# Norms in half-row pieces, second-block constants computed in the last FFN, conditioning rows turned by TensorE, and first projections that start bank by bank

## The reference

```python
def rms_norm(x, g):
    y = x * rsqrt(mean(x * x, -1) + 1e-6)
    return y * g

for l in range(2):                                   # first block
    proj = rms_norm(x, norm_mix_pre[l]) @ w_in[l]    # 1024 -> 3072, four mixers on its slices
    mix = concat([conf, stick_breaking, retention, short_conv]) @ w_out[l]
    x = x + rms_norm(mix, norm_mix_post[l])
    f = conv_ffn(rms_norm(x, norm_ffn_pre[l]), ffn_up[l], ffn_conv_w[l], ffn_down[l])
    x = x + rms_norm(f, norm_ffn_post[l])

mod  = silu(c) @ ada_w + ada_b                       # second block: 6 x 1024 values
modc = silu(c_ctx) @ ada_w + ada_b
u  = rmsnorm(x, norm1_g) * (1 + sc1) + sh1
uc = rmsnorm(ctx, norm1_g) * (1 + sc1c) + sh1c
y  = token_mixer(u, uc, ...)                         # mLSTM and differential attention
x  = x + g1 * y
x  = x + g2 * moe(modulate(rmsnorm(x, norm2_g), sh2, sc2))   # 32 experts, top 4
return rmsnorm(x, final_norm_g)
```

## Time and profile before

| what | value |
|---|---|
| median of 3 runs | 2182.85 us (2179.92 to 2186.36) |
| the profiled execution | 2183.95 us |
| its span | 2182.2 us |
| PE busy | 2061.6 us, 94% of the span |
| DVE, ACT busy | 867.3 us (40%), 595.2 us (27%) |
| mean granted clock of TensorE | 0.981 |
| chain that ended last | PE 78%, DMA 13%, DVE 4%, issue 2%, ACT 2% |
| loads of expert weights | 95 of 4096 KB, 19.0 us each to landing |

### The profile page before, as it was taken

One profiled execution on the slowest core, in us unless ns is written; L12 is line 12 of the kernel. 1 busy time (PEld: TensorE's weight loads), 2 busy tenths in 40 slices (PEclk: granted clock), 3 DMA queues, 4 the chain that ended last, 5 costly groups with the idle time before them and its releaser, 6 DMA issues.

```text
span 2182.2 us, 27676 instructions
## 1 busy us (share of the span) xinstructions
PE 2061.6 (94%) x11094; PEld 1323.7 (61%) x11094; DVE 867.3 (40%) x1510; ACT 595.2 (27%) x962; POOL 11.6 (1%) x23
## 2 busy tenths in 40 slices
PE   8999999999998998899989999999999999999998
PEld 7869998959995776677789533333333333333332
DVE  6847676947675226553622311111111111111111
ACT  4545555445555323342431100000000000000001
POOL 0000000010000000000000000000000000000000
PEclk9999999999998999999999999999999999999999
DMA  7335553355546534021234699999999999999996
GB/s 293 114 135 200 182 174 141 140 171 192 185 163 231 240 148 162 30 78 52 84 116 154 261 413 413 432 432 432 432 431 431 429 431 432 432 432 432 432 432 291
DMA packets 43237, 589.71 MB, mean 270 GB/s; under 512 B 5185, under 2 KB 5873, under 8 KB 9825
## 3 DMA queue, kind: packets, MB, share of 16 engines
q1 hardware_dynamic: 41392, 583.09, 65.5%
q0 software_dynamic: 1456, 5.01, 0.8%
q10 hardware_dynamic: 288, 0.24, 0.0%
HBM read 587.27 MB, written 1.05 MB: 270 GB/s over the span
## 4 chain that ended last, share of the span: by engine, by line
PE 78%; DMA 13%; DVE 4%; issue 2%; ACT 2%; DVEq 0%; SPq 0%; ACTq 0%
PE psum L1869 46%; PE psum L2299 22%; DMA slots<-exp_w_dram 12%; PE psum L2244 3%; PE psum L2336 3%; PE psum L2411 3%; DVE split_weights L1443 1%; DMA slots<-w_in_dram 0%; DMA slots<-ffn_up_dram 0%; DVE work L1569 0%; PE psum L1889 0%; PE psum L2177 0%; DVE work L1586 0%; DVE split_rows L1246 0%; ACT work L1079 0%
## 5 line engine op out<-in xcount | busy, mean ns | idle before, releaser
L2299 PE MATMUL psum<-slots,work 128*64 128x512 f32 x3072 | 687.2, 601 | 47.8 <-DMA slots<-exp_w_dram 46.3
L2299 PEld LDWEIGHTS psum<-slots,work 128*64 128x64 f32 x3072 | 219.9, 138 | 479.8 <-issue 467.1
L1869 PE MATMUL psum<-split_rows,split_weights 128*128 128x256 f32 (+1 forms) x3744 | 489.8, 293 | 13.0 <-DVE split_rows L1495 4.1
L1869 PEld LDWEIGHTS psum<-split_rows,split_weights 128*128 128x128 f32 x3744 | 473.0, 193 | 33.3 <-issue 12.3
L1268 DVE TENSOR_TENSOR split_weights<-slots,split_weights 128x1024 fp32r<-128x1024 f32 x180 | 219.6, 1224 | 161.3 <-ACT split_weights L923 160.6
L923 ACT ACTIVATE split_weights<-slots 128x1024 fp32r<-128x1024 f32 x180 | 189.9, 1058 | 216.7 <-PE psum L1869 179.1
L1869 PE MATMUL psum<-split_weights,split_rows 128*128 128x512 f32 x1008 | 232.3, 390 | 1.0 <-DVE split_weights L1443 1.0
L1869 PEld LDWEIGHTS psum<-split_weights,split_rows 128*128 128x128 f32 x1008 | 188.3, 188 | 42.5 <-issue 2.5
L1831 DVE TENSOR_SCALAR work<-psum 128x512 f32<-128x512 f32 x32 | 22.0, 689 | 401.4 <-PE psum L2299 401.4
L1869 PE MATMUL psum<-work 128*128 128x128 f32 (+9 forms) x964 | 152.7, 335 | 19.9 <-DVE work L1605 7.1
L1869 PEld LDWEIGHTS psum<-work 128*128 128x128 f32 (+2 forms) x964 | 124.3, 196 | 50.4 <-issue 36.9
(11 more groups left out here) (249 smaller groups left out, 1333.3 us busy)
## 6 DMA issues: line engine op xcount, KB each, us to landing
slots<-exp_w_dram SPq DMA_DIRECT2D x95, 4096.0 KB, 19.0
slots<-w_in_dram SPq DMA_DIRECT2D x56, 1024.0 KB, 6.1
slots<-ffn_up_dram SPq DMA_DIRECT2D x44, 1024.0 KB, 4.8
slots<-ada_w_dram SPq DMA_DIRECT2D x24, 1024.0 KB, 7.0
slots<-ffn_down_dram SPq DMA_DIRECT2D x20, 1024.0 KB, 4.9
slots<-w_out_dram SPq DMA_DIRECT2D x12, 1024.0 KB, 5.0
slots<-w_branch_a_dram SPq DMA_DIRECT2D x4, 1024.0 KB, 8.1
slots<-w_branch_b_dram SPq DMA_DIRECT2D x4, 1024.0 KB, 5.0
```

Of the source, the lines that this page charges most:

```text
L1869: return nc.tensor.matmul(out_, lhsT, rhs, start=first, stop=last)
L2299: return nc.tensor.matmul(b[rows, :], lhs[:, rows], rhs, start=first, stop=last, skip_group_check=True)
```

## The change

It has these parts:

1. **No hardware loop.** The two layers are written out (`each_layer`), waits go by constants.
2. **Norms by halves.** The last two `w_out` slots are multiplied for tile 0 first and then tile 1, and the last two units of `ffn_down` bank by bank, so the banks are completed one after another. Squares are taken on 512 columns (`square_of_bank`, `square_of_sum`); the gain is multiplied before the root is known (`times_gain`), and the inverse root, scaling and addition to `x` are one operation (`add_to_x`).
3. **Turned rows by tile, projection by bank.** `turn` writes each tile to its own four banks, `high_rows` and `low_rows` work on 128x128 pieces in `TILE_ORDER`, and the first unit of a projection waits only for the two chunks that it multiplies next.
4. **Work moved into the last FFN.** The silu of the conditioning vectors, the context norm and the products `ada(0)` and `ada(1)` come ahead of the last two units of layer 1's FFN.
5. **Conditioning rows turned.** Rows 0 to 3 and 6 to 9 go through four 128x128 transposes each, and DVE sums the four partial rows (`mod_columns(n)`). `mq` starts at the first of the eight pieces (`u_ready`), with unit splits 1 and 2 placed between the pieces.
6. **Fewer units ahead.** Before a norm only two units of the next stage are split (`MIX_UNITS + 1`), or one (`splits[l + 1](0)`), instead of three.

The diff, cut to its core:

```diff
@@ constants
-LAYER_BANKS = [("T", i, i) for i in range(4)]
+LAYER_BANKS = [("T", i, i) for i in range(8)]
-LAYER_BANKS += [("F", i, i) for i in range(4)]
+LAYER_BANKS += [("F", i, i) for i in range(8)]
+TILE_ORDER = ((0, 0), (1, 0), (0, 1), (1, 1), (2, 0), (2, 1), (3, 0), (3, 1))
@@ every engine
-        def loop_layers(eng, layer):
-            with eng.Fori(0, DEPTH) as l:
+        def each_layer(layer):
+            for l in range(DEPTH):
                 layer(l)
@@ ScalarE
+            def half_square(rows, t, half, l):
+                i = 2 * t + half
+                n_squared[0] += 1
+                nc.scalar.activation(flat(soft)[:, 0:512], rows, ACT.Square, accum_out=half_sumsq[:, i:i + 1]
+                                     ).then_inc(half_squared, 1)
+                act.wait_ge(half_squared, n_squared[0])
+                if half == 0:
+                    nc.scalar.activation(half_mean[:, t:t + 1], half_sumsq[:, i:i + 1], ACT.Identity, bias=EPS, scale=1.0 / D)
...
-                split_until(MIX_UNITS + UNIT_BUFFERS - 1)
-                rms_of_banks(l, "M")
-                rms_of_x(l, 2 * l + 2)
+                split_until(MIX_UNITS + 1)
+                load_root_table()
+                for t in range(TT):
+                    for square in (square_of_bank, square_of_sum):
+                        square("M", l, t, 0)
+                        square("M", l, t, 1)
+                        root(t)
@@ VectorE
+            def times_gain(key, gain, t, squared):
+                for half in (0, 1):
+                    cut = slice(512 * half, 512 * half + 512)
+                    dve.wait_ge(half_squared, squared[half])
+                    step(nc.vector.tensor_tensor(xhat[:, t, cut], psum[:, bank_of((key, 2 * t + half)), :], gain[:, cut], ALU.mult),
+                         0, wait=False)
+            def add_to_x(l, n, key, t):
+                inverse_rms(n, t)
+                for half in (0, 1):
+                    cut = slice(512 * half, 512 * half + 512)
+                    nc.vector.scalar_tensor_tensor(out=x[:, t, cut], in0=xhat[:, t, cut], scalar=rinv[:, t:t + 1],
+                                                   in1=x[:, t, cut], op0=ALU.mult, op1=ALU.add
+                                                   ).then_inc(evacuated[bank_of((key, 2 * t + half))], 1)
...
-                add_normed(l, 1, [("M", i) for i in range(4)], mix_row)
-                normalise(l, 2, 2 * l + 2)
+                for t in range(TT):
+                    times_gain("M", mix_row, t, (16 * l + 4 * t + 1, 16 * l + 4 * t + 2))
+                    add_to_x(l, 8 * l + 2 * t + 3, "M", t)
+                    normalise_tile(8 * l + 2 * t + 4, t)
...
+                for t in range(TT):
+                    times_gain("D", ffn_row, t, (16 * l + 2 * t + 9, 16 * l + 3 * t + 10))
+                    add_to_x(l, 8 * l + t + 7, "D", t)
+                for t in range(TT):
+                    normalise_tile(8 * l + t + 9, t)
@@ TensorE, layer
                     for k in range(KC):
+                        if rows_of and k % 2 == 0:
+                            after_evacuation(pe, (rows_of, k // 2), l)
+                            after_evacuation(pe, (rows_of, 4 + k // 2), l)
...
+                if l == DEPTH - 1:
+                    pe.wait_ge(siluc_ready, 1)
+                    ada_product(0)
+                    ada_product(1)
+                pe.wait_ge(ff_ready, l * 11 + 11)
+                for i in range(4):
+                    t, half = divmod(i, 2)
+                    for n in (len(UNITS) - 2, len(UNITS) - 1):
+                        pe.wait_ge(w_split, l * len(UNITS) + (n + 1))
...
@@ TensorE, block 2
-                            ins = mm(b[:, at_:at_ + 2], rows[:, c * P:(c + 1) * P], cst2("pick")[:, 0:2])
+                            ins = nc.tensor.transpose(b[:, c * P:(c + 1) * P], rows[:, c * P:(c + 1) * P], ident)
...
+                        if first and k % 2 == 0:
+                            pe.wait_ge(u_ready, k // 2 + 1)
@@ VectorE, block 2
+                def mod_columns(n):
+                    k0 = 4 * (n if n < 4 else n - 2)
+                    b = take(dve, ("mT", n), l).rearrange("p (c q r) -> p c r q", c=4, q=4)[:, :, 0:2, :]
+                    m = modT[:, k0:k0 + 4, :]
+                    nc.vector.tensor_reduce(m, b, AX, ALU.add).then_inc(evacuated[bank_of(("mT", n))], 1)
+                    after_evacuation(dve, ("mT", n), l)
+                    step(nc.vector.tensor_tensor(m, m, ada_b[:, k0:k0 + 4, :], ALU.add), l, wait=n in (3, 9))
```

359 lines of the change are left out of this document (193 added, 166 removed).

## The result

The changed kernel takes 2146.07 us (median of 4 runs, 2144.13 to 2146.78); the kernel before took 2183.07 us beside it (4 runs, 2179.92 to 2186.36). The ratio is 0.9829, 95% interval 0.9812 to 0.9846: 1.7% faster, clear of the noise, and within the forecast's range of 2138 to 2151. The profiled executions have spans of 2145.0 and 2182.2 us, 37.2 us apart.

What follows compares the result with a forecast made beforehand. PE's progress ahead of a fixed-length expert-weight stream was taken as the bound, with the seams left to gain. Gains of 16.0 + 7.6 + 12.5 + 2.2 + 1.0 = 39.3 us gave a median of 2144 us, range 2138 to 2151.

Steps and rivals of the forecast that it cites:

- Mixers' ends: At both mixers' ends, tile 0's norm hides under tile 1's products and the projection starts earlier: 8.0 us each, 16.0 together.
- (a): At all four seams, first units run at half clock, costing 7 to 14 us together: 2152 us, chance 0.13.
- Layer 0's end: Behind layer 0's feed-forward, loop wait and table load vanish and the first unit ends at E + 11.5: gain 7.6 us.
- Into block 2: From layer 1's feed-forward to `mk`, bound by the fourth unit's split and the next load: gain 12.5 us.
- (b): At the seams, the norm chain is longer through slower pieces, or `ada(1)`'s load is late: 2155 us, chance 0.12.
- Rows 6 to 9: In block 2's conditioning, transposes replace small `pick` products of 3.41 and 1.84 us: gain 2.2 us.
- 1.5 + 0.7: Split of the 2.2 us gain from turning conditioning rows, with transposes partly at the slow spot.
- Start of layer 0: At layer 0's first projection, only the pieces change and the first unit ends about 20.3 instead of 21.3: gain 1.0 us.
- Expert stage: The stream of expert weights stays as long, about 980 us from first load to end, and only starts earlier: 0 us.
- (c): In seams and layers, pieces take 0.20 us and waits need no computed register, so the chain is shorter: 2134 us, chance 0.09.
- (d): The expert stage waits for something other than PE's progress and takes the gain back: 2183 us, chance 0.03.
- (e): In both written-out layers, engines wait for instructions because code doubles, so the kernel is slower: 2190 us, chance 0.03.

Runs made afterwards that it cites:

- experiment 6: Changed kernel, but block 2's first query product waits for all four pieces of turned rows instead of following piece by piece: 2142.98 us.
- 3: Changed kernel, but the mixer's last eight output products go over both tiles together, as in the kernel before: 2149.63 us.
- experiment 4: Changed kernel, but at the two mixers' ends ScalarE squares each whole tile, not halves: 2148.08 us.
- experiment 2: Changed kernel, but the first unit after each of four norms waits for all eight banks of turned rows to be split: 2156.80 us.
- 1: Kernel before with only the loop removed, both layers written out: 2179.17 us, ratio 0.9978.
- 7: Changed kernel, but the split of `mq`'s fourth unit stands behind the sixth of eight pieces of rows, not the eighth: 2142.94 us.
- experiment 12: Changed kernel, but conditioning rows 6 to 9 are brought to columns by small picking products again, not transposes and a sum: 2155.80 us.
- 5: Changed kernel, but block 2's first two conditioning products and their rows' evacuation stand behind the last feed-forward product again: 2149.62 us.
- 8: Changed kernel with seven instead of five fillers between tile turns at mixers' ends and layer 0's end, plus five short ones in `mq`: 2146.47 us.
- experiment 9: Changed kernel, but at layer 0's start one unit's weights, not three, are split ahead of the turned rows: 2142.93 us.
- 10: Changed kernel with `mq`'s fourth split behind the sixth piece and one unit's weights split ahead of layer 0's first rows: 2139.41 us.
- experiment 11: Changed kernel with the earlier `mq` split, one unit split ahead at layer 0's start, and the extra fillers: 2139.35 us, ratio 0.9805 without one outlier.

## Why the prediction was right

Its total, 2144 against 2146.07 us, is right and so are most of its terms, by their own marks. In part that is luck: the start of layer 0 came out 1.8 us short of its term, and the expert stage gave 1.8 us that were no effect of the change.

- **Mixers' ends** (16.0 forecast, 13.6 measured). The mechanism holds to the mark: turn at E + 5.3, first unit from E + 7.2. The twelve pieces behind the turn came 0.27 us apart, as taken (3.20 us on VectorE). The first unit ended at E + 11.8 where the prediction has 10.5, and before at E + 19.0 where it has 18.5. The loss is the clock: rival (a) came true at these two places. In the profiles where it stayed at 1.00 the first unit ended 1.0 us earlier behind the turn (5.47 against 6.47 us, experiment 6), which gives 8.2 for layer 0. Of each end, the tiles' order is 1.5 us (3), the halves 1.35 (4), the following 2.4 to 3.9 with what the clock did there (2).
- **Layer 0's end** (7.6, measured 7.8). The sum was right, my reading of its parts was not: the loop's issue and table loads, which looked like the largest part, give 2.0 us of start and 0.55 net by themselves (1). The following gives 2.9 (2). The rest, some 3 to 4 us, would be the norm by halves, the products bank by bank and the fewer units split ahead; these were not tried apart.
- **Into block 2** (12.5, measured 11.6). `mk` hung on the fourth split and its load, as said (6, 7): from the last feed-forward product to `mk` it took 36.2 us (685.69 less 649.45), where the prediction has 36.9. What the term left out is the wait of 1.09 us for the second conditioning product's load (part of rival (b)): the two products took 4.86 us (643.85 less 638.99) and not 3.64.
- **Rows 6 to 9** (2.2, measured 3.3, 4.9 by experiment 12). The step "1.5 + 0.7" is right for the products themselves; it left out the conditioning products behind the first of them, which before ran in the stretch at the lower clock: 5.33 us for 32 products at 782.68 us, 3.66 in the kernel after.
- **Start of layer 0** (+1.0, measured -0.8). This step failed. It has the first unit's end at 20.3 us in place of 21.3; it was 22.08 in place of 21.60. The prediction left the clock out here. In the kernel before, six fillers stood behind the turns and TensorE then waited 1.61 us; after the change they are gone and it waits 3.16 us:

```profile
12.78 4.04 PE L1869 MATMUL psum<-const 128*128 128x384 f32 x12
```

  The clock was at its lower level from about 16 to 23 us, and before not at all. The profile of experiment 4, with the same start code, shows the term without that fall: the first unit ends at 20.27 us, as forecast, and the 192 products at 40.4, which would be +1.3.

```profile
16.69 23.70 PE L1940 MATMUL psum<-split_rows,split_weights 128*128 128x256 f32 x192 [3.61 <-DVE split_rows L1300]
20.27 1.06 ACT L957 ACTIVATE split_weights<-slots 128x1024 fp32r<-128x1024 f32 x1 [2.79 <-PE psum L1940]
```

- **Expert stage** (0, measured +1.8). It is a fixed stream, as said. In the profile of before TensorE's first pair ran at the lower clock (6.06 us at 1283.01 for 16 products), in the one after it did not:

```profile
1247.18 3.65 PE L2363 MATMUL psum<-slots,work 128*64 128x512 f32 x16 [0.69 <-ACT work L925]
```

  The stretch from the last 32 products of 128 columns ahead of the experts to the end was 936.7 to 941.9 us over all fourteen profiles, in which that code is the same, so the 1.8 us show no effect of the change.
- **Rivals.** (a) held at three of the seams and cost 1.0 us each at two and nothing at the third, where `mk`'s load hides it; with the start it is about 4 us, not the 8 that I gave it. In the profiles of experiments 5, 8, 9 and 12 the clock fell on `mq`'s last unit too or instead, and `mk` started 18.3 us behind the fourth piece and not 17.4, so there it cost 0.9. Of (b) only the load's wait came. (c), (d) and (e) did not come: the pieces took 0.27 us; from the end of the first 192 products to the tap mark both kernels take 59.2 us, so waits by constants gave nothing and written-out code cost nothing there; and the first expert load came 35.4 us earlier.

## What to carry to other kernels

When work is moved earlier behind a norm, count what stood in the gap: a stretch at the lower clock that cost nothing on constants costs a third of a unit (1.0 of 2.91 us) once real products move into it, and where the constants go away it can come where there was none, as at the start of layer 0. Take a stall apart by undoing one edit at a time and measuring from the nearest mark ahead of it: the parts of an end (order of tiles, halves, following) came to 5.3 to 6.8 of the 6.4 to 7.2 us, while the part that looked largest in the profile (the loop) gave 2.0 us of its 5.2, because the next wait stood right behind it, and 0.55 with the clock's fall. And look at what frees the buffer of the next load: here one split placed two pieces earlier started `mk` 2 us earlier.

## What the runs showed of the hardware

The time of one and the same kernel follows its mean granted clock. The kernel before ran 40 times beside these kernels, at 2174.2 to 2190.1 us, with mean clocks of 0.986 down to 0.979; a straight line through them has 1.9 us for each 0.001 (correlation -0.88). That is about what a busy TensorE would lose: 0.001 of 2182 us is 2.2 us of work, an estimate. The expert stage alone, the same code in every version, differs by up to 5.2 us between profiles. So a difference of a few us between two spans says little, and the marks in the traces told the edits apart.

Where it falls differs between executions of the same code. At the two mixers' ends the kernel after has it at 138.8 to 142.2 and 456.3 to 459.7 us; so have the profiles of experiments 4 and 12, while those of 3, 5, 6, 7, 9 and 10, with the same fillers there, have none. Around 745 and 815 us, at the small products, every profile of the changed kernels has one, and in `mq` every one but that of experiment 11.

What TensorE did ahead of a fall can be set beside it. At the start of layer 0 it waited 3.16 to 5.71 us ahead of the first product in nine profiles, and eight of them have the fall (all but that of experiment 4, with 3.61 us); in the five others (the kernel before and experiments 1, 9, 10 and 11) it waited 1.61 to 1.77 us, and none has it. So the full clock of experiment 9 there goes with its shorter wait. The Trainium skill (TensorE: Matmul & The Clock Gate, Why this matters for your kernels) says that an idle gap brings the lower clock back; the rows agree in part: with waits of 3.38 us ahead of the first units behind a norm, and 5.71 at the start (experiment 2), it fell at all four places, behind 0.80 us in some executions and not in others. What decides between these stays open; two more fillers showed no gain (8, 11).
